# GpSimd's power tables in four parts, and VectorE's order around the first layer's keys, coefficient and attention sums

## The reference

```python
lam = lax.complex(a_re, a_im)                      # 16 groups x 64 states
dt = jnp.exp(log_dt)[:, None]
a_bar = jnp.exp(lam * dt)
b_bar = ((a_bar - 1.0) / lam)[..., None] * b_mat   # the coefficient (a_bar - 1) / lam
...
q = rms_norm(q, q_gain)                            # 64 channels a head
k = rms_norm(k, k_gain)
q = apply_rope(q, cos, sin)
k = apply_rope(k, cos, sin)
...
w = (p[:, :, 0] - lam * p[:, :, 1])                # two softmaxes a head
out = rms_norm(out, sub_gain) * (1.0 - lambda_init)
```

## Time and profile before

| what | value |
|---|---|
| median of 3 runs | 984.04 us (983.65 to 986.6) |
| the profiled execution | 983.3 us, its span 981.5 us |
| PE busy | 954.1 us, 97% of the span |
| DVE busy | 690.5 us, 70% |
| ACT busy | 547.4 us, 56% |
| POOL busy | 263.2 us, 27% |
| first layer's mixing stage | from the start to some 125 us |

### The profile page before, as it was taken

How to read it: one execution, slowest core, us unless ns; L and a number is a source line. 1 busy time by engine, 2 the same in 40 slices (tenths; PEclk the granted TensorE clock), 3 DMA queues, 4 the chain that set the end, 5 groups by cost and what they waited for, 6 DMA issues and landing times.

```text
span 981.5 us, 15775 instructions
## 1 busy us (share of the span) xinstructions
PE 954.1 (97%) x6139; PEld 838.0 (85%) x6143; DVE 690.5 (70%) x1074; ACT 547.4 (56%) x900; POOL 263.2 (27%) x196
## 2 busy tenths in 40 slices
PE   5979999999999999999999999999999999999997
PEld 4867789999978887899999988899777889888886
DVE  6998658776764689676777764558575845666785
ACT  7736556665744656766655654553444454555723
POOL 4891101677800021200555400003131300000030
PEclk9999999999999999999999999999999999999999
DMA  7722355655655552556655566565545445754462
GB/s 287 230 85 87 108 174 191 186 183 174 190 190 154 173 168 86 177 168 194 184 192 183 185 192 194 184 204 175 167 149 150 142 153 169 196 167 152 147 186 84
DMA packets 48473, 165.95 MB, mean 169 GB/s; under 512 B 6544, under 2 KB 7056, under 8 KB 48400
## 3 DMA queue, kind: packets, MB, share of 16 engines
q1 hardware_dynamic: 48400, 164.95, 53.0%
HBM read 162.83 MB, written 1.05 MB: 167 GB/s over the span
## 4 chain that ended last, share of the span: by engine, by line
PE 86%; DVE 8%; ACT 2%; POOL 1%; issue 1%; DMA 0%; DVEq 0%; POOLq 0%; SPq 0%; ACTq 0%
PE PJ L605 14%; PE PJ L607 13%; PE PJ L606 13%; PE PJ L596 10%; PE PJ L598 10%; PE PJ L597 10%; DVE wlo L1710 2%; PE PJ L557 2%; PE PJ L559 2%; PE PJ L558 2%; PE T L1045 1%; PE T L1036 1%; PE S L652 1%; DVE ropeq L1821 1%; PE T L974 1%
## 5 line engine op out<-in xcount | busy, mean ns | idle before, releaser
L1710 DVE TENSOR_TENSOR wlo<-raw,whi 128x1024 fp32r<-128x1024 f32 x294 | 366.9, 1280 | 87.1 <-ACT whi L1104 84.8
L1104 ACT ACTIVATE whi<-raw 128x1024 fp32r<-128x1024 f32 x294 | 302.5, 1062 | 73.6 <-DMA raw<-weights_in 64.7
L596 PE MATMUL PJ<-xthb,whi 128*128 128x256 f32 x864 | 243.1, 281 | 0.9 <-DVE wlo L1710 0.5
L598 PE MATMUL PJ<-xthb,wlo 128*128 128x256 f32 x864 | 242.3, 280 | 0.0
L597 PE MATMUL PJ<-xtlb,whi 128*128 128x256 f32 x864 | 241.5, 280 | 0.0
L605 PE MATMUL PJ<-whi,xthb 128*128 128x512 f32 (+1 forms) x432 | 174.3, 403 | 3.6 <-DVE wlo L1710 3.6
L607 PE MATMUL PJ<-whi,xtlb 128*128 128x512 f32 (+1 forms) x432 | 167.9, 389 | 0.0
L606 PE MATMUL PJ<-wlo,xthb 128*128 128x512 f32 (+1 forms) x432 | 167.7, 388 | 0.0
L596 PEld LDWEIGHTS PJ<-xthb,whi 128*128 128x128 f32 x864 | 163.0, 189 | 1.7 <-issue 1.5
L597 PEld LDWEIGHTS PJ<-xtlb,whi 128*128 128x128 f32 x864 | 163.0, 189 | 0.2
L598 PEld LDWEIGHTS PJ<-xthb,wlo 128*128 128x128 f32 x864 | 162.9, 189 | 0.0
(11 more groups left out here) (402 smaller groups left out, 1342.1 us busy)
## 6 DMA issues: line engine op xcount, KB each, us to landing
raw<-weights_in SPq DMA_DIRECT2D x294, 512.0 KB, 3.5
rt<-bmerge_in SPq DMA_DIRECT2D x6, 256.0 KB, 4.4
xres<-x_in SPq DMA_DIRECT2D x2, 512.0 KB, 5.5
memx<-mem_in SPq DMA_DIRECT2D x2, 512.0 KB, 4.1
y_out<-xn SPq DMA_DIRECT2D x4, 256.0 KB, 2.3
rowv<-rows_in SPq DMA_DIRECT2D x1, 576.0 KB, 10.5
ptmp<-bexp_in SPq DMA_DIRECT2D x2, 256.0 KB, 6.3
cex<-cexp_in SPq DMA_DIRECT2D x2, 256.0 KB, 8.5
```

The source lines that it names most:

```text
L596: pe.matmul(o, a, xh[:, k, :], start=(first and f % 2 == 0), stop=False, skip_group_check=True)
L598: m = pe.matmul(o, b, xh[:, k, :], start=False, stop=last, skip_group_check=True)
L1104: act.activation(whi[:, p % HIGHS, :], raw[:, p % LOADS, :], ACT.Copy).then_inc(hi_ready, 1)
L1710: dve.tensor_tensor(wlo[:, p % LOADS, :], raw[:, p % LOADS, :], whi[:, p % HIGHS, :].bitcast(F32), ALU.subtract).then_inc(lo_ready, 1)
```

## The change

- `output_powers` and `input_powers` take `parts`. With `parts=4`, as the first layer now calls them, each instruction over 8 state tiles becomes four over 2 tiles, 256 or 192 elements a partition instead of 1024 or 768. The second layer's calls keep whole instructions, so do the two plain copies.
- On POOL `head_powers(0, 1)` now stands ahead of `folded(0)`.
- The coefficient: 1 / |lam|^2 and the two products with it are worked out at DVE's start, in seven instructions behind `par_ready` 2 and ahead of the first `norm_scale`. `coefficients()` has six instructions instead of 15 and stands behind `head_sums(1)` instead of behind pair 9. The order of the two negated rows is swapped, and `fold_coefficient` reads them so.
- DVE scales the keys right behind their rotary product. `phase_turns` comes behind that and pair 12.
- Pairs 15 and 16 are split ahead of `lambdas()`.
- In both layers `diff_sums(1)` stands ahead of `diff_norm(0)`, and the split of pair 22 in between goes behind `diff_norm(1)`, to that of pair 23.

The diff, unchanged lines cut:

```diff
@@ -376,7 +376,7 @@
...
             eng.wait_ge(sem("cex_landed"), 16 * (l + 1))
-            cr, ci, nci, ncr = (wide(sp_[:, r, 8 * l:8 * l + 8], 32, 2) for r in (9, 10, 11, 12))
+            cr, ci, nci, ncr = (wide(sp_[:, r, 8 * l:8 * l + 8], 32, 2) for r in (9, 10, 12, 11))
             re, im = cex[:, 0, :, :], cex[:, 1, :, :]
...
@@ -385,34 +385,43 @@
...
 
-        def output_powers(eng, link, l, c, tmp, steps=(0, 1, 2)):
-
-            ar, ai = (wide(apw[:, c, 1:STEP + 1, 8 * l:8 * l + 8].rearrange("p t s -> p s t"), 32, 3) for c in range(2))
-            cr, nci = (wide(gpw[:, c, :, 0, :], STEP, 2) for c in range(2))
+        def output_powers(eng, link, l, c, tmp, steps=(0, 1, 2), parts=1):
+
             t = tmp.rearrange("p (s t h) -> p s t h", s=ST, t=STEP)
-            i0, k0, i1, k1, op = ((cr, ar, nci, ai, ALU.add), (nci, ar, cr, ai, ALU.subtract))[c]
-            o = gpw[:, c, :, 1:STEP + 1, :]
-            if 0 in steps:
-                link(eng.tensor_tensor(o, i0, k0, ALU.mult), False)
-            if 1 in steps:
-                link(eng.tensor_tensor(t, i1, k1, ALU.mult))
-            if 2 in steps:
-                link(eng.tensor_tensor(o, o, t, op))
-
-        def input_powers(eng, link, l, c, x, tmp, steps=(0, 1)):
-
-            ar, ai = (wide(apw[:, k, 1:STEP, 8 * l:8 * l + 8].rearrange("p t s -> p s t"), 32, 3) for k in range(2))
-            br, bi = (wide(bex[:, k, :, :], STEP - 1, 2) for k in range(2))
+            w = ST // parts
+            for step in steps:
+                for at in range(0, ST, w):
+                    ar, ai = (wide(apw[:, k, 1:STEP + 1, 8 * l + at:8 * l + at + w].rearrange("p t s -> p s t"), 32, 3) for k in range(2))
+                    cr, nci = (wide(gpw[:, k, at:at + w, 0, :], STEP, 2) for k in range(2))
+                    i0, k0, i1, k1, op = ((cr, ar, nci, ai, ALU.add), (nci, ar, cr, ai, ALU.subtract))[c]
+                    o, tt_ = gpw[:, c, at:at + w, 1:STEP + 1, :], t[:, at:at + w, :, :]
+                    if step == 0:
+                        link(eng.tensor_tensor(o, i0, k0, ALU.mult), False)
+                    if step == 1:
+                        link(eng.tensor_tensor(tt_, i1, k1, ALU.mult), at + w == ST)
+                    if step == 2:
+                        link(eng.tensor_tensor(o, o, tt_, op), at + w == ST)
+
+        def input_powers(eng, link, l, c, x, tmp, steps=(0, 1), parts=1):
+
             xv = x.rearrange("p (s t h) -> p s t h", s=ST, t=STEP)
             t = tmp[:, 0:ST * 96].rearrange("p (s t h) -> p s t h", s=ST, t=STEP - 1)
-            o = xv[:, :, 1:STEP, :]
-            i1, k1, op = (bi, ai, ALU.subtract) if c == 0 else (br, ai, ALU.add)
+            w = ST // parts
             if 0 in steps:
                 link(eng.tensor_copy(xv[:, :, 0, :], bex[:, c, :, :]), False)
-                link(eng.tensor_tensor(o, br if c == 0 else bi, ar, ALU.mult), False)
+            for step in ([0] if 0 in steps else []) + ([1, 2] if 1 in steps else []):
+                for at in range(0, ST, w):
+                    ar, ai = (wide(apw[:, k, 1:STEP, 8 * l + at:8 * l + at + w].rearrange("p t s -> p s t"), 32, 3) for k in range(2))
+                    br, bi = (wide(bex[:, k, at:at + w, :], STEP - 1, 2) for k in range(2))
+                    i1, k1, op = (bi, ai, ALU.subtract) if c == 0 else (br, ai, ALU.add)
+                    o, tt_ = xv[:, at:at + w, 1:STEP, :], t[:, at:at + w, :, :]
+                    if step == 0:
+                        link(eng.tensor_tensor(o, br if c == 0 else bi, ar, ALU.mult), False)
+                    if step == 1:
+                        link(eng.tensor_tensor(tt_, i1, k1, ALU.mult), at + w == ST)
+                    if step == 2:
+                        link(eng.tensor_tensor(o, o, tt_, op), at + w == ST)
             if 1 in steps:
-                link(eng.tensor_tensor(t, i1, k1, ALU.mult))
-                link(eng.tensor_tensor(o, o, t, op))
                 eng.sem_inc(sem("xpow_ready"), 1)
...
@@ -1590,8 +1599,8 @@
...
             pool.wait_ge(sem("bex_ready"), 1)
-            input_powers(pool, link, 0, 0, x_tile(0), ptmp)
-            input_powers(pool, link, 0, 1, x_tile(1), ptmp)
+            input_powers(pool, link, 0, 0, x_tile(0), ptmp, parts=4)
+            input_powers(pool, link, 0, 1, x_tile(1), ptmp, parts=4)
             head_powers(0, 0)
...
@@ -1601,10 +1610,10 @@
...
             link(pool.tensor_copy(ident4.rearrange("p (t h) -> p t h", t=STEP), wide(skip[:, 0:32], STEP)))
+            head_powers(0, 1)
             folded(0)
-            head_powers(0, 1)
-            output_powers(pool, link, 0, 0, ptmp)
-            output_powers(pool, link, 0, 1, ptmp)
+            output_powers(pool, link, 0, 0, ptmp, parts=4)
+            output_powers(pool, link, 0, 1, ptmp, parts=4)
             pool.sem_inc(sem("gpow_ready"), 1)
...
@@ -1756,6 +1765,14 @@
...
             dve.sem_inc(sem("par_ready"), 1)
+            are, aim = col("are"), col("aim")
+            link(dve.tensor_tensor(v[16], are, are, ALU.mult), False)
+            link(dve.tensor_tensor(v[17], aim, aim, ALU.mult))
+            link(dve.tensor_tensor(v[16], v[16], v[17], ALU.add))
+            link(dve.reciprocal(v[13], v[16]))
+            link(dve.tensor_tensor(v[16], are, v[13], ALU.mult), False)
+            link(dve.tensor_tensor(v[15], aim, v[13], ALU.mult), False)
+            link(dve.tensor_tensor(v[17], aim, v[13], ALU.mult))
             norm_scale(0, xres, 0)
...
@@ -1766,7 +1783,6 @@
...
             dve.sem_inc(sem("par_ready"), 1)
-            v[15] = apw[:, 1, 1, :]
             lo_upto(3)
...
@@ -1784,22 +1800,14 @@
...
 
-                are, aim = col("are"), col("aim")
-                link(dve.tensor_scalar(v[14], apw[:, 0, 1, :], -1.0, None, ALU.add))
-                link(dve.tensor_tensor(v[16], are, are, ALU.mult))
-                link(dve.tensor_tensor(v[17], aim, aim, ALU.mult))
-                link(dve.tensor_tensor(v[16], v[16], v[17], ALU.add))
-                link(dve.reciprocal(v[16], v[16]))
-                link(dve.tensor_tensor(v[17], v[14], are, ALU.mult))
-                link(dve.tensor_tensor(v[18], v[15], aim, ALU.mult))
-                link(dve.tensor_tensor(v[17], v[17], v[18], ALU.add))
-                link(dve.tensor_tensor(v[9], v[17], v[16], ALU.mult))
-                link(dve.tensor_tensor(v[17], v[15], are, ALU.mult))
-                link(dve.tensor_tensor(v[18], v[14], aim, ALU.mult))
-                link(dve.tensor_tensor(v[17], v[17], v[18], ALU.subtract))
-                link(dve.tensor_tensor(v[10], v[17], v[16], ALU.mult))
-                link(dve.tensor_scalar(v[11], v[10], -1.0, None, ALU.mult))
-                link(dve.tensor_scalar(v[12], v[9], -1.0, None, ALU.mult))
+
+                from_one = apw[:, :, :, :].rearrange("p c t n -> p (c t) n")[:, 0:STEP + 3:STEP + 2, :]
+                link(dve.tensor_scalar(apw[:, 0, 0, :], apw[:, 0, 1, :], -1.0, None, ALU.add))
+                link(dve.tensor_tensor(sp_[:, 22:24, :], from_one, sp_[:, 16:18, :], ALU.mult), False)
+                link(dve.tensor_tensor(sp_[:, 13:15, :], from_one, sp_[:, 15:17, :], ALU.mult))
+                link(dve.tensor_tensor(v[9], v[22], v[23], ALU.add), False)
+                link(dve.tensor_tensor(v[10], v[14], v[13], ALU.subtract))
+                link(dve.tensor_scalar(sp_[:, 11:13, :], sp_[:, 9:11, :], -1.0, None, ALU.mult))
                 dve.sem_inc(sem("par_ready"), 1)
...
@@ -1904,24 +1912,22 @@
...
                 rotary(0, A, "q_terms", "q_rot", s0 + (10 if l else 9))
-                if l == 0:
-                    lo_upto(s0 + 10)
-                    coefficients()
                 lo_upto(s0 + 11)
...
                 head_sums(1)
+                if l == 0:
+                    coefficients()
                 rotary(1, B, "k_terms", "k_rot", s0 + (14 if l else 12))
-                if l == 0:
-                    phase_turns(dve, link, 0)
-                    lo_upto(s0 + 13)
                 dve.wait_ge(sem("hr_ready"), 2 * l + 2)
...
                 if l == 0:
+                    lo_upto(s0 + 13)
+                    phase_turns(dve, link, 0)
                     dve.wait_ge(sem("mixw_landed"), 32)
...
@@ -1967,8 +1973,8 @@
...
                     batch_max(0)
+                    lo_upto(s0 + 17)
                     lambdas()
-                    lo_upto(s0 + 17)
                     scans()
...
@@ -2008,9 +2014,8 @@
...
                     lo_upto(s0 + 22)
+                diff_sums(1)
                 diff_norm(0)
-                lo_upto(s0 + 23)
-                diff_sums(1)
                 diff_norm(1)
...
```

## The result

The changed kernel takes 987.09 us (median of 14 runs, 985.52 to 989.3); the kernel before, run beside it, 983.42 us (14 runs). The ratio is 1.0034 with a 95% interval from 1.0027 to 1.0041. So the change makes the kernel slower by 3.7 us. The forecast of 985.8 us had the sign and the main mechanism, the long wait for GpSimd at the Toeplitz products; the time lies in its range and 1.3 us above it. One of its own signs of being wrong came too, a wait of over 2 us at the second input transposes. Its likeliest case, "within 0.3%", is missed narrowly: 0.34%, with the bound inside the interval.

What follows compares the result with a forecast made beforehand. PE, busy 954.1 of 981.5 us, was taken as the bound, so only its gaps counted. Toeplitz products +1.7, low clock +1.8 and attention sums -1.7 gave +1.8 on 984.0: 985.8 us, range 979.5 to 990.5.

Steps and rivals of the forecast that it cites:

- Four parts, own cost 4.8 us: GpSimd's power tables: pieces add 4.8 us for the output powers and 2.5 us for the input powers.
- Exclusion, instruction by instruction: GpSimd and VectorE on shared SBUF ports: the second waits for the other's whole instruction; VectorE's pairs cost GpSimd about 1.0 us.
- Rival C: GpSimd keeps the ports over its four pieces, VectorE waits as before, only the attention sums pay: 982.3 us, chance 0.12.
- rival A: GpSimd isn't held up: output powers end near 72.8, no long wait or low clock, 977.5 us, chance 0.22.
- Take off the two idle times of the chain: GpSimd's chain to the output powers: idle of 1.82 us for queries' sums and 1.23 us for the coefficient goes, -3.05 us.
- The order of keys' root and fold costs nothing by itself: GpSimd ahead of the output powers: the sum over both stays the same, the keys' root comes some 8 us sooner.
- VectorE's instructions newly between pieces: GpSimd's chain to the output powers: pairs 15 and 16, two scans and small instructions now run in this stretch, +5.4 us.
- The end of the powers, 79.9: GpSimd's last output power ends at 79.9 instead of 72.77, so PE could start the Toeplitz products at 80.0.
- Second input transposes, 0.7 us: PE loses 0.7 us waiting for input powers ending at 36.8, swallowed later; over 2 us would show the forecast wrong.
- rival B: GpSimd's pieces starve behind several VectorE instructions: Toeplitz products start at 82.7 to 83, 988.8 to 990.5 us, chance 0.30.
- PE's arrival 72.7, stall 7.3: PE reaches the Toeplitz products at 72.7 and waits 7.3 us for GpSimd, replacing three stalls that sum to 5.2.
- Low clock +1.8, up to 2.9: Behind PE's long wait the Toeplitz products run at the lower clock level: +1.8 us, up to +2.9 if it lasts longer.

Runs made afterwards that it cites:

- e1_whole: The changed kernel with input and output powers in whole instructions again, all the rest of the change kept; 981.0 us, ratio to before 0.9975.
- e11_fold_first: e1_whole with the fold put ahead of the keys' root on GpSimd again, as in the kernel before; 987.6 us, ratio to before 1.0043.
- e3_in_whole: The changed kernel with whole input powers, output powers still in four parts; 985.7 us, ratio to before 1.0025.
- e2_out_whole: The changed kernel with whole output powers, input powers still in four parts; 983.3 us, ratio to before 0.9997.
- e5_busy: The changed kernel plus 60 transposes on PE, results overwritten, in its wait ahead of the Toeplitz products; 985.3 us, ratio to before 1.0019.
- e10_old_parts: The kernel of e4_sums with input and output powers in four parts, engine orders otherwise old; 983.9 us, ratio to before 1.0008.
- e4_sums: The kernel before with only the attention sums moved ahead of the first norm and pair 22's split behind both norms; 980.8 us, ratio 0.9974.
- e7_late: The changed kernel with the Toeplitz products behind pair 16 on PE instead of ahead of it; 985.0 us, ratio to before 1.0019.
- e6_two: The changed kernel with whole input powers and output powers in two parts instead of four; 981.4 us, ratio to before 0.9980.

## Why the prediction was right or wrong

*Four parts, own cost 4.8 us: right as far as it can be seen.* Four undisturbed output pieces last 0.4 us more than the whole (0.36 forecast), and so do four input pieces, 1.96 us (line 419 in the change) where the whole one lasts 1.52 to 1.57 (lines 419 and 421 in e1_whole). The third instruction's pieces never ran four in a row undisturbed.

*Exclusion, instruction by instruction: right.* Beside the pieces one VectorE instruction of 1024 elements takes 1.2 to 1.8 us, where pair 14's low half took 2.98 beside whole powers, and GpSimd pays. Rival C falls by this, the parts do let VectorE in; rival A falls by the last power at 81.14, not near 73.

*"Take off the two idle times of the chain", -3.05 us: measured -0.8.* From the end of the input powers to the start of the output powers it was 22.19 us and is 21.36. The 1.82 us ahead of the queries' root went as forecast: the sums end at 32.29 instead of 35.05, ahead of GpSimd's own arrival. That hangs on the input parts; in e1_whole, with whole input powers, the sums end at 35.24 and the 1.82 us are still there. The idle time for the coefficient went too, but 1.24 us for the keys' sums came in its place. VectorE couldn't give these sooner, since it had itself idled 2.62 us for ACT's squares; I had booked the gain without asking what VectorE waits for next.

*"The order of keys' root and fold costs nothing by itself": wrong.* e1_whole and e11_fold_first differ in this order alone. The output powers start at 58.94 us in the one and here in the other:

```profile
54.61 1.97 POOL L399 TENSOR_TENSOR gpw<-gpw,apw 128x1024 f32<-128x1024 f32 x1
```

With the keys' root first, the identity's two scalings take 2.96 us instead of 1.40 and the fold 7.5 (51.40 to 58.86) instead of 5.4, because they now run beside VectorE's work on the keys, its splits and the phases. In the change the fold lasts 7.5 too, and the output powers start at 59.31, where my terms give 55.51 + 2.5 + 1.0 - 3.05 = 56.0. Beside VectorE's new order it is worth its price all the same: without it PE loses 6.6 us (e11_fold_first).

*VectorE's instructions newly between pieces, +5.4 us: too large.* The stretch of output powers grew from 17.3 to 21.8 us, 4.6 where 2.3 + 5.4 was forecast; of it about 2.3 to 2.5 is own cost and 2.1 to 2.3 VectorE.

*The end of the powers, 79.9: measured 81.14, close by luck in part.* The inputs came 1.1 us later than their line says (37.95, not 36.8), the two steps above lost 2.2, the output stretch was 3.1 shorter, and 1.0 is a slip of the sum: it leaves out the "one more pair" that the inputs' own line counts. Errors of 4.3 us one way and 3.1 the other leave 1.2.

*Second input transposes, 0.7 us: measured 2.2.* This is over the 2 us that I had named as a sign of being wrong, and points to rival B, whose wait there was over 3; the 81.34 lies between my 80.0 and B's 82.7. No piece in the first layer waited for five VectorE instructions as in the earlier trace rows: the worst group, four pieces in 5.47 us, has the two scans and pair 17's split beside it, one behind each piece, and its longest piece lasts 1.70 us. So B's starving did not show in this stage. The Trainium skill (SBUF — State Buffer, "SBUF: two separate sides") has the engine that comes second blocked for the other's whole instruction; with that the 1.70 us agree, and the earlier trace rows stay the exception. B's upper end of 990.5 doesn't follow from its terms, which give 988.8 and 1.1 for the longer low clock (2.9 in place of 1.8), 989.9.

*The waits for keys and pair 14 go: right*; pair 15 costs 0.34 and not 0.7. *PE's arrival 72.7, stall 7.3: measured 73.75 and 7.6*, right in kind. PE came a good microsecond later because of the inputs (+1.5), and the wait for GpSimd did swallow that: e3_in_whole comes at 71.6 and starts only 0.8 us sooner than the change. It isn't swallowed where the powers are not late, as in e2_out_whole.

*Low clock +1.8, up to 2.9: measured 2.8* (e5_busy), the upper end. The row I took it from was a wait of 3.15 us; after 7.59 us the low level lasted nearly through the whole block.

*Attention sums -1.7: measured -2.1.* *Nothing in the second layer: right*, by the constant 867.5 to 868.1.

The sum: Toeplitz products +3.1 (forecast +1.7), clock +2.8 (+1.8), sums -2.1 (-1.7), together +3.8 against +1.8; the spans differ by 3.7. The time came closer than this difference, 1.3 us off and not 2, because the 984.0 that I started from was the median of three runs and 14 runs give 983.4; that is luck too.

## What to carry to other kernels

Where two engines exclude each other, cutting one engine's instruction into pieces moves time from one chain to the other and adds the pieces' own cost. By these runs it pays only if the engine that gets in has someone waiting for it right then, and the engine that is cut has slack up to its own consumer: here VectorE idled for ACT with what it won, while PE waited for GpSimd. Change parts one by one before joining them: three reordered lines held the whole gain, and the parts hid it.

## What was not expected of the hardware

With the input powers in four parts the runs of one kernel fall into groups. e10_old_parts has 981.1 and 981.2, then six runs from 983.6 to 984.0, then four from 985.5 to 986.2; e4_sums, the same kernel without parts, has all seven from 980.6 to 981.2. e7_late spreads from 982.5 to 987.2, e2_out_whole from 981.4 to 985.5; e1_whole from 980.6 to 981.5. The kernel before, with whole powers, isn't free of it (982.4 to 984.6, and one of 14 at 986.6). In the profiled executions PE's wait at the second input transposes was 0.7, 2.15 and 2.6 us in e7_late, e5_busy and e2_out_whole, which have the same lists on all engines up to there. That more boundaries leave more to small shifts in who comes first fits this; it was not tested.

The clock's price depended on the length of the wait, and on what followed: 2.8 us behind 7.6 us of waiting in the change, 1.6 behind 3.6 us in e6_two, where removing it brought nothing.
